# Modulation sums moved between engines, splits on GpSimd, and weights laid out chunk by chunk, in a four-layer diffusion backbone step

## The reference, cut to what matters

```
def ada_modulation(cond, w, b):            # w: (2048, 6144) per layer, 4 layers
    m = silu(cond) @ w + b
    shift, scale, gate = split(m, 3)
...
h = rms_norm(x, norm_pre[l]) * (1 + scale) + shift
out = mixer(h)                              # projections of 2048 rows, attention or scans
x = x + rms_norm(out, norm_post[l]) * gate
```

## Time and profile before

| | |
|---|---|
| median of 3 runs | 3222.21 us |
| lowest, highest | 3212.88, 3223.43 us |
| the profiled execution: its time, its span | 3231.19 us, 3229.1 us |
| TensorE busy (matmuls, 19631 records) | 3059.2 us, 95% |
| VectorE busy | 1908.1 us, 59% |
| ScalarE busy | 1050.1 us, 33% |
| GpSimd busy | 203.9 us, 6% |
| mean DMA rate | 197 GB/s |
| granted TensorE clock, mean | 0.975 |

### The profile page before, as it was taken

How to read it: one execution, slowest core, us unless ns; L and a number is a source line. 1 busy time by engine, 2 the same in 40 slices (tenths; PEclk the granted TensorE clock), 3 DMA queues, 4 the chain that set the end, 5 groups by cost and what they waited for, 6 DMA issues and landing times.

```text
span 3229.1 us, 46744 instructions
## 1 busy us (share of the span) xinstructions
PE 3059.2 (95%) x19631; PEld 2651.0 (82%) x19631; DVE 1908.1 (59%) x2811; ACT 1050.1 (33%) x1409; POOL 203.9 (6%) x321
## 2 busy tenths in 40 slices
PE   5799999999999999889998999999999999999998
PEld 2588889977788989779987877987787999987777
DVE  3499985545767734638775363764475775235443
ACT  1333333233324222232324243324324222323332
POOL 1034340000000210000000000000000000000000
PEclk7899999999999999989999999999999999999999
DMA  9889995411455897866654564555363655431132
GB/s 354 323 309 352 344 334 182 164 49 53 156 183 179 246 257 270 334 244 219 226 183 142 178 220 164 200 205 191 129 226 126 212 196 176 131 95 53 53 131 91
DMA packets 290498, 636.01 MB, mean 197 GB/s; under 512 B 22000, under 2 KB 55424, under 8 KB 281584
## 3 DMA queue, kind: packets, MB, share of 16 engines
q1 hardware_dynamic: 264384, 524.58, 47.4%
q0 software_dynamic: 25904, 108.44, 9.7%
HBM read 561.01 MB, written 71.89 MB: 196 GB/s over the span
## 4 chain that ended last, share of the span: by engine, by line
PE 80%; DMA 7%; DVE 7%; ACT 3%; DVEq 2%; issue 1%; ACTq 1%; POOL 0%; SPq 0%; POOLq 0%
PE bank L347 36%; PE bank L351 21%; DMA raw<-in_ada_w 3%; PE bank L881 3%; PE bank L875 3%; PE bank L386 2%; PE bank L896 2%; DVE w_lo L501 2%; DVE arena L2147 1%; PE bank L922 1%; PE bank L2518 1%; DMA raw<-in_mla_w_in 1%; PE bank L412 1%; DMA raw<-in_s_w_in 1%; PE bank L900 1%
## 5 line engine op out<-in xcount | busy, mean ns | idle before, releaser
L501 DVE TENSOR_TENSOR w_lo<-raw,w_hi 128x2048 fp32r<-128x2048 f32 (+2 forms) x352 | 617.7, 1771 | 697.7 <-ACTq L495 694.2
L494 ACT ACTIVATE w_hi<-raw 128x2048 fp32r<-128x2048 f32 (+2 forms) x352 | 520.4, 1496 | 1246.8 <-PE bank L347 612.7
L347 PE MATMUL bank<-hT_hi,w_hi 128*128 128x384 f32 (+1 forms) x2608 | 898.4, 344 | 22.3 <-ACT scratch L981 7.7
L347 PE MATMUL bank<-hT_lo,w_hi 128*128 128x384 f32 (+1 forms) x2608 | 885.9, 340 | 0.0
L347 PE MATMUL bank<-hT_hi,w_lo 128*128 128x384 f32 (+1 forms) x2608 | 885.8, 340 | 0.0
L347 PEld LDWEIGHTS bank<-hT_hi,w_hi 128*128 128x128 f32 (+1 forms) x2608 | 492.5, 189 | 49.9 <-issue 34.3
L347 PEld LDWEIGHTS bank<-hT_lo,w_hi 128*128 128x128 f32 (+1 forms) x2608 | 492.5, 189 | 1.5 <-issue 0.5
L347 PEld LDWEIGHTS bank<-hT_hi,w_lo 128*128 128x128 f32 (+1 forms) x2608 | 492.2, 189 | 1.4 <-issue 0.6
L351 PE MATMUL bank<-w_hi,hT_hi 128*128 128x512 f32 x1056 | 421.9, 399 | 3.1 <-issue 2.9
L351 PE MATMUL bank<-w_hi,hT_lo 128*128 128x512 f32 x1056 | 418.1, 396 | 0.0
L351 PE MATMUL bank<-w_lo,hT_hi 128*128 128x512 f32 x1056 | 417.9, 396 | 0.0
(11 more groups left out here) (338 smaller groups left out, 2922.1 us busy)
## 6 DMA issues: line engine op xcount, KB each, us to landing
raw<-in_ada_w SPq DMA_DIRECT2D x192, 1024.0 KB, 7.3
raw<-in_mla_w_in SPq DMA_DIRECT2D x64, 768.0 KB, 7.5
raw<-in_gla_w_in SPq DMA_DIRECT2D x48, 1024.0 KB, 7.4
raw<-in_mla_w_in SPq DMA_DIRECT2D x40, 1024.0 KB, 5.3
raw<-in_mla_w_out SPq DMA_DIRECT2D x32, 1024.0 KB, 5.2
raw<-in_s_w_in SPq DMA_DIRECT2D x32, 1024.0 KB, 8.6
s_out_dram<-arena POOLq DMA_DIRECT2D x32, 512.0 KB, 5.8
s_in_dram<-arena POOLq DMA_DIRECT2D x16, 1024.0 KB, 9.6
```

What stands on the lines that cost most here:

```text
L347: mm = nc.tensor.matmul(banks[m][0:width, 0:TOK], wp[:, k, at:at + width], hp[:, kt, :], start=(first and n == 0), stop=(last and n == 2))
L494: nc.scalar.activation(dst, src_, ACT.Copy)
L501: nc.vector.tensor_tensor(dst, src_, pick(w_hi, *part)[0], ALU.subtract)
```

## The change

1. The groups of the modulation multiplied on TensorE go from 27 to 16 (0 to 15). Groups 16 to 47 are summed on VectorE, in nine sets of 3 or 4 groups (`summed_sets`), each set spread evenly over a run of dense chunks: 4 steps per chunk beside `gate0`, `out0`, `out1`, `out2`, 4.3 beside `glu1`, 2.1 to 2.7 beside `u1`/`gate1`, the two halves of GLA and `q3`.
2. These sums now run along rows. The host hands over the matrix transposed, `ada_rows`: 32 output columns x 4 input-row quarters on the partitions, 512 input rows along the free dimension. The conditions' silu values, written once to DRAM, are broadcast over the partitions (`pool_silu`, four DMAs from GpSimd, six times), and one instruction multiplies a row tile with them and adds up the products into one column (`accum_out`). The product itself goes to bank 5 or over `raw` and is not read. For the sets beside GLA and `out2` the second condition's row lies in bank 4 instead of SBUF.
3. `pe_ada_take` is one step per set: 4 matmuls with a 128 x 32 matrix `spread` that adds the four quarters.
4. The `w_lo` split of 74 chunks moves from VectorE to GpSimd: chunks 1 to 15 of `gate0`, `out0`, `out1`, `out2`, and 2 to 15 of `glu1` (`by_pool`). GpSimd's own DMAs and waits stand between them in its order.
5. All weight matrices except the narrow `krope` and `glr` ones are rearranged by the host, so that each chunk is contiguous: 8 KB per partition in one run (6 KB in the q jobs) instead of 4 runs of 2 KB.

The core of the diff:

```diff
+ADA_TENSOR = 16
+def summed_sets(layers):
...
+    return [(range(16, 20), chunks("gate0", 0, 16), (13824, 14336, 22144)),
+            (range(20, 23), chunks("out0", 1, 13), (12928, 13632, 13448)),
+            (range(23, 27), chunks("u1", 1, 16) + chunks("gate1", 0, 11), (4608, 5120, 5632)),
+            (range(27, 31), chunks("glu1", 1, 16), (19200, 19712, 20224)),
+            (range(31, 34), chunks("out1", 1, 13), (12928, 13632, 13448)),
+            (range(34, 38), gla[:24], (12928, None, 13448)),
+            (range(38, 41), gla[28:47], (12928, None, 13448)),
+            (range(41, 44), chunks("out2", 1, 13), (12928, None, 13448)),
+            (range(44, 48), chunks("q3", 1, 31), (9216, 9728, 10240))]
...
-                if before == "ada" and n in SUMMED and q < 3:
-                    sp.wait_ge(ada_summed, 32 * SUMMED.index(n) + 8 * (q + 1))
-                elif before == "ada" and n in SUMMED:
-                    sp.wait_ge(ada_turned, turned_with(n))
+                if before == "ada" and n >= ADA_TENSOR:
+                    sp.wait_ge(ada_summed, sums_before(n) + 8 * (q + 1))
...
+        def pe_ada_take(pe, f):
...
+            for k in range(4):
+                mm = nc.tensor.matmul(banks[5][32 * k:32 * k + 32, 0:n], spread[:, :], sums_of(f)[:, k, 0:n],
+                                      start=True, stop=True, skip_group_check=True)
...
         def dve_ada_step(a, k):
...
+            for o in (2 * (k % 4), 2 * (k % 4) + 1):
+                kk, c = ((0, 0), (1, 0), (0, 1), (2, 0), (1, 1), (3, 0), (2, 1), (3, 1))[o]
+                done = sums_before(a) + 8 * s + o
+                if done > (o != 1):
+                    nc.vector.wait_ge(ada_summed, done - (o != 1))
...
+                nc.vector.scalar_tensor_tensor(out=got if c else banks[5][:, :], in0=got, scalar=1.0, in1=silu_of(f, c), op0=ALU.mult,
+                                               op1=ALU.mult, accum_out=sums_of(f)[:, kk, at:at + 1]).then_inc(ada_summed, 1)
...
+        def pool_silu(pool, r):
...
+            for q in range(4):
+                nc.gpsimd.dma_start(to[32 * q:32 * q + 32, :, :],
+                                    silu_dram[:, q * GC:(q + 1) * GC].unsqueeze(0).broadcast_to([32, 2, GC])).then_inc(silu_in, 16)
...
+            elif eng == "pool":
+                nc.gpsimd.wait_ge(hi_ready, n + 1)
+                nc.gpsimd.wait_ge(lo_ready, n)
+                for part in parts:
+                    dst, src_ = pick(w_lo, *part)
+                    nc.gpsimd.tensor_tensor(dst, src_, pick(w_hi, *part)[0], ALU.subtract).then_inc(lo_ready, 1)
...
+        def by_pool(n):
+            name, g, s = dense[n] if n >= 0 else ("", 0, 0)
+            return 4 * g + s >= {"gate0": 1, "out0": 1, "glu1": 2, "out1": 1, "out2": 1}.get(name, 99)
...
+                if l != layers[-1]:
+                    pool_splits(f"out{l}", 1, 2)
                 fetch_x(pool, l)
+                if l != layers[-1]:
+                    pool_splits(f"out{l}", 2, 16)
...
+def by_chunk(weights, cols=GC):
+    layers, _, n = weights.shape
+    parts = weights.reshape(layers, 4, 4, P, n // cols, cols).transpose(0, 4, 1, 3, 2, 5)
+    return np.ascontiguousarray(parts)
```

More of the change, by code:

```diff
@@ L101, in ada_after, with chunks @@
 def ada_after(layers):
[L103 to L116, removed]
+    return {("q0", g): ADA_START + g for g in range(ADA_TENSOR - ADA_START)}
+def summed_sets(layers):
+    def chunks(name, first, end):
+        per = chunks_of(name)
+        return [(name, n // per, n % per) for n in range(first, end)]
+    gla = [(f"{name}2", n, s) for name, groups in GLA_ORDER for n in range(groups) for s in range(4)]
+    return [(range(16, 20), chunks("gate0", 0, 16), (13824, 14336, 22144)),
[7 more added lines that the diff above has]
+            (range(44, 48), chunks("q3", 1, 31), (9216, 9728, 10240))]
+SILU_PLACED = {0: 0, 1: 1, 2: 2, 3: 3, 4: 4, 8: 5}
 def dense_order(layers):
@@ L123, in summed_steps @@
 def summed_steps(layers):
-    steps, takes, loads, dense = {}, {}, {}, dense_order(layers)
-    for groups, pace, keys in summed_apart(layers):
+    steps, loads, dense = {}, {}, dense_order(layers)
+    for groups, keys, _ in summed_sets(layers):
         for n, a in enumerate(groups):
             for k in range(16):
-                key = keys[(16 * n + k) // pace]
+                key = keys[(16 * n + k) * len(keys) // (16 * len(groups))]
                 steps.setdefault(key, []).append((a, k))
@@ new lines, in dve_ada_step, with dve_ada_take @@
+            if k == 15 and a == SETS[f][0][-1]:
+                nc.vector.drain().then_inc(ada_summed, 1)
+        def dve_ada_take(f):
+            groups, at = SETS[f][0], 0
+            nc.vector.wait_ge(ada_turned, set_taken(f))
+            for l in range(DEPTH):
+                j = [4 * (a % ADA_LAYER) for a in groups if a // ADA_LAYER == l]
+                if j:
+                    tt = dve_ada_add(l, j[0], j[-1] + 4, at)
+                    at += j[-1] + 4 - j[0]
+            tt.then_inc(ada_turned, 1)
@@ L502, in split_chunk, with pool_splits @@
                 nc.vector.drain().then_inc(lo_ready, 1)
+        def by_pool(n):
+            name, g, s = dense[n] if n >= 0 else ("", 0, 0)
+            return 4 * g + s >= {"gate0": 1, "out0": 1, "glu1": 2, "out1": 1, "out2": 1}.get(name, 99)
+        def pool_splits(name, first, end):
+            for n in range(first, end):
+                split_chunk("pool", name, n // 4, n % 4)
         def split_next(eng, name, g):
             n = chunk(name, g, chunks_of(name) - 1) + 1 if name else 0
-            if n < len(dense):
+            if n < len(dense) and not (eng == "dve" and by_pool(n)):
                 split_chunk(eng, *dense[n])
```

251 lines of the change are left out of this document (152 added, 99 removed).

## The result

| | kernel before | changed kernel |
|---|---|---|
| median of the runs, us | 3217.55 (4 runs) | 3259.76 (4 runs, 3256.35 to 3262.11) |
| profiled execution, us | 3231.2 | 3260.2 |
| its span, us | 3229.1 | 3258.4 |

A forecast was written before the change was run, and what follows sets the result against it. TensorE, busy 95% of the span, was taken to bound the kernel, with DMA full at the start and in `q0`. Terms -61 - 31 - 4 + 20 + 5 - 4 - 3 = -78 gave 3145 us, 8-in-10 range 3095 to 3285.

The forecast's parts named there:

- Splits on GpSimd: 74 chunks' splits: 4.5 us each on GpSimd, done 6.4 us after the slot came free, under 8.4: hidden, cost 0.
- needs 7.7 of 8.47: Beside `gate0`: with the split gone, VectorE's load per chunk in us against the chunk's length, so the sums fit.
- Rival 1: `gate0`, outs, `glu1`: VectorE's two-SBUF-operand sums and GpSimd's splits exclude each other; 3240 to 3340, likely 3285; chance 0.27.
- rival 2: All new sums: with an accumulator they run at half rate, 1.22 us each; about +205 against 98, 3330; chance 0.04.
- Loss 20: GLA layer: VectorE can't fit the sums, 14 us in `va` plus 6 in chunks before and after it.
- The 28 that 5 groups gain there: GLA layer: the saving on TensorE from 5 groups leaving it, 28 us, set against a loss of 20.
- the 61 of the sum: Modulation leaving TensorE: 11 groups go, 44 quarters of 1.18 us (52) and 11 turns of 0.79 (9), gain 61.
- Count of records: TensorE's modulation lines: line 386 falls from 864 to 512 records, the take from 336 to 72.
- The take: 21 takes of 1.68 us replaced by nine of 0.5 each, gain 31; the ring's wait gives 4 more.
- A sum with accumulator: VectorE's new sums: 0.81 us each, 0.66 plus 0.15 for writing out one column.
- Runs of 8 KB: Contiguous weight chunks count only where DMA is full: gain 4 us at the start and 3 in `q0`.
- The order of GpSimd's queue: Around `out` starts and in `gate0`, DMAs and waits stand between GpSimd's splits: cost 5 us, 0 to 10.

The follow-up runs named there:

- silu in the banks: Changed kernel, GpSimd splits kept, silu copied into PSUM banks 4 and 5 for the five sets meeting those splits, unused product to the arena: 3171.01 us, ratio 0.9881.
- hT at the old place: Changed kernel with silu read from PSUM banks, tile `spread` declared behind `scratch` so hT lies as in the kernel before: 3212.13 us, ratio 0.9997.
- dead tile: Kernel before with an unused 32-column tile ahead of the arena, moving hT by 128 bytes: 3180.21 us, ratio 0.9896; with the chunk layout too: 3172.95 us.

## Why the prediction was wrong

**The sum as the runs give it**, medians of their comparisons: layout -5 (its run); move of hT -35 (3172.95 against 3207.93); new sums, takes and splits with nothing blocked -2 (3171.01 against 3172.95; no difference); blocked sums +89 (3259.76 against 3171.01). Together 47, and the measured difference is 42. The medians come from different comparisons; by the ratios the four are -5, -37, +4 and +81, together 43, and the +4 has about 12 us either way. The forecast had -7, nothing, -71 and nothing for them.

**The step that failed is "Splits on GpSimd ... hidden, cost 0"**, with its companion that VectorE "needs 7.7 of 8.47" and all fits. The price of a split was well taken (4.5 against 4.63 to 4.75), and it did lie beside other work; but it cannot lie beside a sum with two SBUF operands, and the same 8.4 us of a chunk were given to VectorE and to GpSimd, as if side by side. Rival 1 described it rightly, mechanism and place. It forecast 1.7 to 3 us on 65 chunks; 89 us are 1.4 on each of them. It was too dear because it charged VectorE with the whole 4.5 us of every split: 56 blocked sums and 222 us are 3.0 a split, and with 3.0 in place of 4.5 its 11.0 us beside `gate0` becomes 9.5, 1.0 over the 8.47 of a chunk. The other splits met a copy out of a bank, a sum with a bank operand, or a VectorE that had nothing to do. Its lower end of 3240 doesn't follow from its own sum, 3145 + 110 = 3255; and in rival 2 the outs' 10.7 against 8.39 over 36 chunks give 83, not 45. It got 0.27, and "no row shows an exclusion" was counted against it although the trace had no GpSimd arithmetic beside anything: a view that cannot show a thing is no evidence against it.

**"Loss 20" in the GLA layer was the other mis-sized term**, and the saving it was set against was mis-sized too. The layer between the same marks, with the layout alone, then with silu in the banks and hT at the old place (same placement, nothing blocked):

```profile
1762.80:2315.40 552.60, 547.95 (x3009) 449.45 (x3005) 293.80 (x354) 192.37 (x217) 12.43 (x17) 1.00 0.49 184
```

```profile
1749.50:2333.00 583.50, 529.46 (x2701) 449.08 (x2701) 372.62 (x708) 188.95 (x210) 15.06 (x17) 0.94 0.41 150
```

TensorE's idle time goes from 4.7 to 54.0 us, 49 lost against 20 forecast. I had looked at `va`, where chunk stands beside chunk, and priced the units' chunks at 6 together; 38 us are waited in the four units, where a stream of sums stands before the one operand that TensorE needs.

"The 28 that 5 groups gain there" left out two groups. Seven leave TensorE in this layer, 39 us by the prediction's own prices, and with the cheaper takes 43 (the 61 of the sum counts all eleven groups and stands). The records agree, 308 fewer where the count gives 312. But TensorE's busy time falls by 18.5 only (23.7 in the pair with hT moved), mostly because its clock falls: 0.94 instead of 1.00. The first matmuls of a unit with the layout alone, then behind a wait of some 10 us in the other version, and the stretch in which these stand:

```profile
1921.53 0.85 PE bank L1437 x24
1922.38 0.69 PE bank L1442 x12
```

```profile
1918.46 1.55 PE bank L1528 x24
1920.00 1.28 PE bank L1533 x12
```

```profile
1909.90:1927.00 17.10, 8.54 (x52) 6.61 (x53) 10.31 (x27) 1.68 (x5) 0.00 (x0) 0.50 0.17 62
```

The granted clock is 0.50 there, the lower of the two levels (1.2 GHz), and it fell while TensorE stood idle in that wait; the same matmuls take 1.8 times as long. TensorE is busy for 46.5 us of this layer at that level, against 3.0 with the layout alone; as dense matmuls of 384 columns follow each other in 320 ns at it and in 175 otherwise, I estimate 20 us for it. No term of the prediction has the clock. So the layer, forecast at -43 + 20 = -23, came out at +31.

Over the whole kernel TensorE's busy time falls by 76 between the kernel before and the version with hT at the old place, and its idle time grows by 62: the change's idea comes out at nothing. Against the layout alone the idle time grows by 71, of which 22 lie outside the GLA layer; what they wait for was not taken apart.

**Point by point.** Count of records: right (512 of line 390, 72 of the take). The chain beside `gate1` without its pieces: 8.52 for 48 matmuls of which some wait, 8.47 forecast. The take: 0.19 us for 8 records, 0.5 forecast, so the better price was the one from the S5 rows. A sum with accumulator: forecast 0.81; the next starts 0.61 later, whether its product goes to SBUF or to a bank, and 0.79 only where both products go to the same bank and the program makes the second wait for the first's end (`o == 1` in `dve_ada_step`, one sum of eight). That is 0.64 on average, no more than the 0.66 without an accumulator; the write-out's records of 80 and 140 ns cost nothing of their own. Rival 2, half rate with two fp32 operands in SBUF, falls, and with it, for this instruction, the sentence of the Trainium skill (Vector Engine (DVE) Microarchitecture Reference, Points that are easy to get wrong): 697 ns with two, 682 with one. Runs of 8 KB: forecast 4 and 3, measured 5 in all (ratio 0.9984); in the one pair of executions 8 at the start, of which 4 are left at attention. The order of GpSimd's queue, forecast 5: TensorE's wait for gates at the outs is 12.7 us in three cases, but 11.7 in two with nothing blocked, so the queue itself isn't separated from the rest. The place of hT: not seen; no row of the kernel before could show it.

## What to carry to other kernels

Before work is moved from VectorE to GpSimd, look at what VectorE does beside it: with two operands in SBUF the two take turns, with one of them in PSUM they don't, and copying one operand over once a stage costs next to nothing. An engine that waits rarely can still lose what it saves when its partner has a single urgent result queued behind bulk work; look at the waits at such heads, not at the mean of the stretch. Such a wait can cost more than its length, as the matmuls behind it may run at the lower clock. And measure a change against the old kernel with the new kernel's memory layout, since a dead tile alone was worth 1%.

## What was not expected of the hardware

- Moving hT by 128 bytes in SBUF makes every dense matmul 2 to 2.6% (weights from hT) and 1.2 to 1.5% (hT streamed) quicker to follow the last, 33 us here (ratio 0.9896); 64 and 192 bytes bring 9 and 15 us in a single run each, by way of one kind or the other.
- A GpSimd split of 2048 columns takes 4.63 us beside sums with an operand in PSUM and 4.75 beside blocked ones: GpSimd is held up by some 0.5 us at most by a sum, and a blocked sum by up to 4.4, 4.0 on average over 56.
- A sum of 128x512 with an accumulator lets the next start after 0.61 us, whether its product goes to a PSUM bank or to SBUF. The 0.79 us seen between two sums with products in the same bank go with a wait in the program.
- The same 18927 matmuls keep TensorE busy for 2933.5 us at a mean granted clock of 0.97 and for 2960.0 at 0.956.

The fastest kernels measured that leave nothing out are the version with silu in the banks (3171), its siblings with six (3169) and five groups (3166) in `u1` and `gate1`, and the kernel before with layout and dead tile alone (3173); they can't be told apart. Keeping the GLA layer's groups on TensorE and the rest as with silu in the banks was not tried.
